# One load moved to a second queue and one copy moved ahead of two reductions

## The reference, cut to what matters

```python
h = rmsnorm(x, g_pre_mix)                    # x: (1024, 1024)
proj = h @ w_in + b_in                       # split into aq, ak, av, bq, bk, bv
out_a = mixer_a(aq, ak, av, sinks, t5_bias)  # 8 query heads, 2 key heads, window of 128, softmax with a sink
out_b = mixer_b(bq, bk, bv, rel_table)       # 8 heads, own chunk of 64 and 8 chunks before it
y = concat(out_a, out_b) @ w_out
x = x + rmsnorm(y, g_post_mix)
h = rmsnorm(x, g_pre_mlp)
y = square(relu(h @ w_up)) @ w_down
out = x + rmsnorm(y, g_post_mlp)
```

## Time and profile before

| | us |
|---|---|
| median of 3 runs | 1059.54 (1059.53 to 1059.8) |
| the profiled execution's own time | 1059.02 |
| its span | 1057.2 |
| TensorE matmul busy | 1047.8 (99%) |
| VectorE busy | 767.5 (73%) |
| ScalarE busy | 478.1 (45%) |

### The profile page before, as it was taken

One profiled execution on the slowest core, in us unless ns is written; L12 is line 12 of the kernel. 1 busy time (PEld: TensorE's weight loads), 2 busy tenths in 40 slices (PEclk: granted clock), 3 DMA queues, 4 the chain that ended last, 5 costly groups with the idle time before them and its releaser, 6 DMA issues.

```text
span 1057.2 us, 16366 instructions
## 1 busy us (share of the span) xinstructions
PE 1047.8 (99%) x5765; PEld 870.2 (82%) x5765; DVE 767.5 (73%) x1633; ACT 478.1 (45%) x984; POOL 213.2 (20%) x191
## 2 busy tenths in 40 slices
PE   9999999999999999999999999999999999999997
PEld 7899888787887888888888888888888888888886
DVE  5854577667678656888997877876544677778997
ACT  6532355554558655855413113122244444454562
POOL 1400000000000000319767657564100000000000
PEclk9999999999999999999999999999999999999999
DMA  9450111110125123215544443445777733354344
GB/s 254 116 187 7 47 60 27 61 46 21 46 49 172 66 95 124 76 46 196 187 180 160 154 155 140 159 160 192 236 244 243 235 116 99 123 187 158 100 133 166
DMA packets 81744, 138.01 MB, mean 131 GB/s; under 512 B 17640, under 2 KB 34032, under 8 KB 79616
## 3 DMA queue, kind: packets, MB, share of 16 engines
q1 hardware_dynamic: 80976, 136.78, 39.7%
q10 hardware_dynamic: 688, 0.20, 0.1%
HBM read 98.93 MB, written 42.51 MB: 134 GB/s over the span
## 4 chain that ended last, share of the span: by engine, by line
PE 97%; issue 1%; DVE 1%; ACT 1%; DVEq 0%; POOL 0%; ACTq 0%; POOLq 0%
PE ps L1863 27%; PE ps L1865 27%; PE ps L1864 27%; PE ps L1990 3%; PE ps L2056 3%; PE ps L2020 3%; PE ps L2041 1%; PE ps L2014 1%; PE ps L2171 1%; PE ps L2173 1%; PE ps L2159 1%; PE ps L2189 1%; PE ps L1875 1%; PE ps L2039 1%; PE ps L2012 0%
## 5 line engine op out<-in xcount | busy, mean ns | idle before, releaser
L1863 PE MATMUL ps<-b_hi,wc_hi 128*128 128x512 f32 x448 | 174.8, 390 | 0.0
L1865 PE MATMUL ps<-b_hi,wc_lo 128*128 128x512 f32 x448 | 174.4, 389 | 0.0
L1864 PE MATMUL ps<-b_lo,wc_hi 128*128 128x512 f32 x448 | 174.4, 389 | 0.0
L1863 PE MATMUL ps<-tm_hi,sm_hi 128*128 128x512 f32 x448 | 174.3, 389 | 0.0
L1864 PE MATMUL ps<-tm_lo,sm_hi 128*128 128x512 f32 x448 | 174.3, 389 | 0.0
L1865 PE MATMUL ps<-tm_hi,sm_lo 128*128 128x512 f32 x448 | 174.3, 389 | 0.0
L1260 ACT ACTIVATE sm_hi<-sm_raw 128x512 fp32r<-128x512 f32 x112 | 70.7, 631 | 162.4 <-DMA sm_raw<-u_matrices 162.4
L1788 DVE TENSOR_TENSOR sm_lo<-sm_raw,sm_hi 128x512 fp32r<-128x512 f32 x112 | 77.4, 691 | 78.4 <-ACT sm_hi L1260 77.8
L1863 PEld LDWEIGHTS ps<-b_hi,wc_hi 128*128 128x128 f32 x448 | 84.1, 188 | 18.2 <-DVE wc_lo L1575 0.5
L1864 PEld LDWEIGHTS ps<-tm_lo,sm_hi 128*128 128x128 f32 x448 | 84.1, 188 | 17.6
L1865 PEld LDWEIGHTS ps<-b_hi,wc_lo 128*128 128x128 f32 x448 | 84.1, 188 | 17.6
(11 more groups left out here) (226 smaller groups left out, 2131.7 us busy)
## 6 DMA issues: line engine op xcount, KB each, us to landing
u_matrices<-stage SPq DMA_DIRECT2D x112, 256.0 KB, 2.0
sm_raw<-u_matrices SPq DMA_DIRECT2D x112, 256.0 KB, 2.6
up_raw<-in_w_up SPq DMA_DIRECT2D x16, 1024.0 KB, 5.0
w<-in_w_down SPq DMA_DIRECT2D x64, 256.0 KB, 3.8
w_raw<-in_w_in SPq DMA_DIRECT2D x8, 512.0 KB, 3.5
xr<-in_x SPq DMA_DIRECT2D x8, 512.0 KB, 3.5
x_rows<-xr SPq DMA_DIRECT2D x8, 512.0 KB, 2.6
xf<-x_rows SPq DMA_DIRECT2D x8, 512.0 KB, 3.5
```

The source lines that it names most:

```text
L1863: pe.matmul(out, w_hi_, x_hi_, start=start, stop=False)
L1864: pe.matmul(out, w_hi_, x_lo_, start=False, stop=False)
L1865: return pe.matmul(out, w_lo_, x_hi_, start=False, stop=stop)
```

## The change

The load of column 0's second half goes from SyncE's queue, where it was third, to ScalarE's queue, where it is first, ahead of the three loads of the first weights. In step 34 VectorE's `copies_of(33)` goes from behind `normalize` of step 34 to ahead of the minima of step 35. Nothing is computed otherwise.

```diff
@@ load_x, SyncE's queue
                 else:
                     sp.dma_start(xraw[:, 0, 0:4], src[:, 0:4]).then_inc(s_in[0], 16)
                     sp.dma_start(g1, g_pre_mix).then_inc(s_g1, 16)
-                    sp.dma_start(xraw[:, 0, 4:8], src[:, 4:8]).then_inc(s_x0, 16)
@@ ScalarE's program
         def _(act):
+            act.dma_start(xraw[:, 0, 4:8], x[4 * P:8 * P, 0:P].rearrange("(t p) n -> p t n", p=P)).then_inc(s_x0, 16)
             load_first_weights(act, 0)
@@ VectorE's attention steps
                 if n >= LATE:
                     copies_of(n - 1)
+                if n == A_STEPS + 2:
+                    copies_of(n - 1)
                 if paired(n) and n % T == 2:
                     scores(n + 1)
                 if n < STEPS and not (paired(n) and n % 2):
                     for hh in range(2):
                         normalize(n, hh)
-                if 1 <= n < LATE and not paired(n - 1):
+                if 1 <= n < LATE and not paired(n - 1) and n != A_STEPS + 2:
                     copies_of(n - 1)
```

## The result

The changed kernel takes 1064.05 us (median of 6 runs, 1062.82 to 1065.17) against 1059.53 (6 runs, 1059.0 to 1059.8): 4.5 us slower, ratio 1.0043 with a 95% interval of [1.0032, 1.0053]. The forecast was 1059.2, range 1058.7 to 1060.6. The profiled execution is the longest of the six: 1065.17 us, span 1063.1, so 5.9 us over the span before.

A forecast was written before the change was run, and what follows sets the result against it. TensorE, busy 1047.8 of 1057.2 us, was taken as the bound. The copy's -0.5 us and the head's +0.2 us made -0.3 us, from 1059.54 to 1059.2 us, range 1058.7 to 1060.6.

The forecast's parts named there:

- The copy: Attention, step 34: moving VectorE's copy earlier removes TensorE's wait before weigh(33), gaining 0.5 us, with nothing new late behind it.
- What the load removes: Head: TensorE's 0.21 us wait for column 0's second half goes, but becomes part of a longer wait, worth 0.
- What the two halves share: Head: column 0's first half lands 0.3 us later beside the second, between 0 and 0.8; head cost 0.2 us.
- the empty stretch of rows 7: Head, 1.50 to 2.25 us: engines nearly empty at 53 GB/s; using it could take back 0.6 us of sharing.
- Rival 1: Head: halves share evenly and weights come late as well; net +0.4 us, so 1059.9; chance 0.25.
- The weights share too: Head: first weights land between 5.43 and 6.2 us against a need at 6.06; no cost taken, up to 0.2 us in range.
- The 0.8 us: Head: most that column 0's first half could be delayed by sharing with its second half and the first weight load.
- what the change adds: Head: loads on ScalarE's queue move back one issue, hidden; those on SyncE's move up 0.43 us, and none was late.
- the sum: Whole kernel: -0.5 us in the attention and +0.2 us in the head make -0.3 us, so 1059.2 us.
- Rival 2: Head: idle TensorE loses its quick clock, 2.15 us of work takes twice as long, so 1061.4; chance 0.08.
- The range: Whole kernel: 1058.7 to 1060.6 us, the high end taking in late, evenly sharing halves and part of a clock fall.

The follow-up runs named there:

- e9: Kernel before, with the second half alone on ScalarE's queue and the first weights on SyncE's queue ahead of column 1, copy not moved: 1059.52 us, ratio 0.9998.
- e4: Changed kernel with the three first-weight loads issued by SyncE's queue ahead of column 1, only the second half on ScalarE's: 1058.66 us, ratio 0.9993.
- e5: Changed kernel with 24 more idle transposes behind the transposes of column 0, so TensorE works through the wait: 1061.51 us, ratio 1.0019.
- e2: Kernel before with only the second half's load moved to ScalarE's queue, copy left as before: 1063.05 us, ratio 1.0036.
- e6: Changed kernel with ScalarE's queue in the other order, the three first-weight loads and then the second half: 1063.23 us, ratio 1.0034.
- e3: Changed kernel with SyncE's queue holding column 1 and all behind it until column 0's first half has landed: 1059.28 us, ratio 0.9999.
- e7: Changed kernel with two small loads moved up on SyncE's queue, so column 1 is issued behind all three weight loads: 1060.08 us, ratio 1.0009.
- e8: Changed kernel with the first weights' two query loads in 512-byte pieces, half as many, same bytes; output not the reference's: 1062.44 us, ratio 1.0027.

## Why the prediction was wrong

**The copy: right.** The gain of 0.5 us was measured as 0.52 (4.89 to 4.37), VectorE did not wait for its input, and nothing new was late behind it.

**What the load removes: right.** The wait for the second half went and was worth about 0: e9 has no harm beside it and takes 1059.52 us against 1059.38.

**What the two halves share: wrong in sign, and small.** The forecast had the first half land 0.3 us later. It landed at 0.75 + 3.3 = 4.05, 0.2 us earlier than before, and the first transposes started at 4.22 and not 4.42. That the empty stretch of rows 7 was enough for both is likely and not shown. e4 and e9 start them at 4.14 and 4.28. Rival 1 (the halves share evenly and the first is late) did not occur; it also had the weights late, at a price of 0.2 us.

**The step that failed** is "The weights share too: bounds for their landing are 5.43 and 5.43 + 0.8 = 6.2 ... I take no cost". Measured: 9.4, and 7.96 to 8.15 in e5 and e2; a wait of TensorE of 3.69 us stood where the sum had nothing. The 0.8 us were those of the first half, lent to another transfer with other neighbours. Under what the change adds stood what was missing: everything on SyncE's queue moves up, called harmless because nothing there was late. The question asked was only whether those loads would profit. Column 1 is 512 KB, and it moved from 2.27 to 1.79 at the same time as the weights moved from 1.20 and 1.68 to 1.87 and 2.4 and behind 256 KB on their own queue. Before, the weights had only the halves of column 0 beside them in their stretch; after, they had column 1. The packets by queue (q1 is SyncE's, q10 ScalarE's) show it, from 3 to 4 us in the kernel before, when most of the weights' packets went:

```profile
q1 hardware_dynamic: 467, 0.16, 61.2%
q10 hardware_dynamic: 499, 0.12, 54.5%
```

and 4.4 to 6.4 us in the changed kernel, a stretch twice as long:

```profile
q1 hardware_dynamic: 1015, 0.51, 89.1%
q10 hardware_dynamic: 278, 0.07, 15.3%
```

499 packets in one microsecond then, 278 in two now, while the engines were nearly as busy (116% and 104%). In e6 the second half, last on ScalarE's queue, gets less than half of the packets too:

```profile
q1 hardware_dynamic: 798, 0.40, 77.7%
q10 hardware_dynamic: 365, 0.19, 33.8%
```

That the loads of SyncE's queue from column 1 on are a cause is shown by e3 (hold them: loss gone) and e4 (weights in front of them on their own queue: loss gone); column 1 was not held apart from what stands behind it. That the place behind the second half is needed too is shown by e6, where the weights, first on their queue again, land in 3.2 us although column 1 is issued at 1.79. Why ScalarE's queue gets a fifth to a third of the packets and not half is not shown, and e7, whose engines were not full, says that a division of the engines' time is not the whole of it.

**The second part of the cost is the clock.** Rival 2 had the mechanism and its price about right (2.15 us for one stretch, measured 2.83, and 1.5 to 1.6 in e2 and e6), at 0.08. Its condition was taken from the idle pieces under 1 us that the forecast expected; with a wait of 2.3 us (e2) or 3.7 the condition was another. e5 takes this part away by itself. The Trainium skill, "TensorE: Matmul & The Clock Gate", part 1, says that an idle stretch brings the slow level back. The rows agree in the changed kernel (0.82 from 8 to 10 us, 0.50 behind it), in e2 and in e6, and e8 shows a wait of 2.86 us without a fall. In e2 and e6 the clock fell only after TensorE had gone back to work: e2's reads 1.00 from 8.8 to 9.5 us, with the first products at 8.82, and 0.55 from 9.5 to 10; e6's reads 1.00 from 8.0 to 8.5, with TensorE back at 8.14, and 0.50 from 8.8 on.

**The range** left out every way in which the first weights could be later than the first half. From the rows of before the bound was to be had: columns 0 and 1 and the weights are 262 x 2 + 524 + 197 = 1245 KB, and if the weights come last of these, at rows 7's 309 GB/s from 2.25 on, that is 2.25 + 4.0 = 6.3, and 0.4 us more from the last packets to the landing (before, ScalarE's queue had none after 4.6 and the last weight load landed at 4.98), 6.7. Even that is under 9.4: this bound takes the engines as full and the weights as last of these loads only, and neither held (228 GB/s from 4 to 5 us in the changed kernel, and later loads of SyncE's queue went ahead of the last 17 packets).

## What to carry to other kernels

When a load is moved from one queue to another, list for both queues what is issued in which order and when, and for each load what is in flight beside it: here the load behind the inserted one and the load that moved up were the ones that collided. Put what is needed first in front of the large load on the same queue (e4); a place on another queue did not protect it. A wait in a stretch of TensorE's own work is paid a second time when it brings the clock down (1.5 to 2.8 us here), and cheap idle work (e5: 24 transposes, a median 2.5 us lower) saves that second payment only. And a wait read from one trace is one draw: a late bunch of 17 packets made 1.3 us of difference between two profiles of the same head.

## What was not expected of the hardware

- Two queues in flight did not get equal parts: from 4.4 to 6.4 us ScalarE's got 278 of 1293 packets, nearly all in 256-byte pieces (changed kernel), and 365 of 1163 in 512-byte pieces (e6). The engines need not be full for it: share 0.74 in e7.
- The same loads in the same order let `first_hi(0)` start at 7.96, 8.15 and 9.44 us in three profiles (e5, e2, changed kernel). The 9.44 hung on the last 17 packets.
- Two 256 KB loads started together on two queues landed within 0.5 us of each other (4.05 and 4.5), and the one on the chain landed no later than with the small weight loads beside it (4.25).
- The clock fell after TensorE had been idle for 2.27 us (e2) and did not with 2.86 us (e8), in one profile each. In e8's profile the array had also reached the quick level sooner: the first four transposes took 0.61 us, against 1.09 in e2.
